# Two mixing stages reordered: the place of GLA's exponent, of three projections and of GLA's norm, and the release of attention's score banks

## What is computed

```python
x = x + 0.5 * mx[2] * swiglu(modulate(rms_norm_2(x), mx[0], mx[1]), ffn1_w1[l], ffn1_w3[l], ffn1_w2[l])
hx = modulate(rms_norm_2(x), mx[3], mx[4]) @ w_in[l]
hz = modulate(rms_norm_2(z), mz[3], mz[4]) @ w_in[l]
mix_x, mix_z = token_mixing(hx, hz, ..., not last)
x = x + mx[5] * (mix_x @ w_out[l])
x = x + 0.5 * mx[8] * swiglu(modulate(rms_norm_2(x), mx[6], mx[7]), ...)   # z likewise, if not last

def token_mixing(...):            # four mixers, 256 of the 1024 channels each
    a_x = fourier_mix(px['fourier'])                     # 2D FFT over tokens and 64 channels, real part
    b_x = neighborhood_attention(na_q, na_k, na_v, kz_na, vz_na, na_rpb)   # 4 heads of 64, window + context, bias
    ox_gla, _, _ = bidir_gla(*gla_prepare(px, *gates), s_f, s_b)   # gated linear attention, both directions
    c_x = gla_output(ox_gla, px['gla_r'], gla_norm)      # rms norm over a head, times silu(r)
    d_x = block_attention(qx_gqa, keys of x and z, values of x and z)      # 4 heads, 2 kv heads, rope
    return concatenate([a_x, b_x, c_x, d_x])             # in layer 0 the same for z
```

## Time and profile before

| | us |
|---|---|
| median of three runs | 3559.2 |
| lowest, highest | 3558.4, 3567.6 |
| the profiled execution | 3562.57 |
| its span, first to last instruction | 3560.7 |
| TensorE busy | 3386.7 |
| VectorE, ScalarE, GpSimd busy | 1622.9, 580.0, 43.8 |
| mean granted clock of TensorE | 0.977 |

### The profile page before, as it was taken

One profiled execution on the slowest core, in us unless ns is written; L12 is line 12 of the kernel. 1 busy time (PEld: TensorE's weight loads), 2 busy tenths in 40 slices (PEclk: granted clock), 3 DMA queues, 4 the chain that ended last, 5 costly groups with the idle time before them and its releaser, 6 DMA issues.

```text
span 3560.7 us, 41820 instructions
## 1 busy us (share of the span) xinstructions
PE 3386.7 (95%) x16652; PEld 2770.6 (78%) x16652; DVE 1622.9 (46%) x3349; ACT 580.0 (16%) x1208; POOL 43.8 (1%) x48
## 2 busy tenths in 40 slices
PE   8999999999999999999999778999999999987999
PEld 7887888888888888788885444688888888664888
DVE  4667223145682232365563643564656556344100
ACT  2121112111211021100003234100011000233100
POOL 0000000000000000000000010000000000020000
PEclk9999999999999999999999889999999999998999
DMA  5777557636775476333322120232322323231454
GB/s 185 216 201 237 170 155 208 165 101 190 213 234 191 145 210 179 93 83 95 83 90 59 52 38 24 63 109 66 95 83 71 107 68 98 55 84 29 130 157 116
DMA packets 655631, 440.69 MB, mean 124 GB/s; under 512 B 24336, under 2 KB 654512, under 8 KB 655312
## 3 DMA queue, kind: packets, MB, share of 16 engines
q1 hardware_dynamic: 652416, 430.28, 41.8%
q0 software_dynamic: 1552, 6.07, 1.0%
q10 hardware_dynamic: 1472, 1.68, 0.1%
HBM read 436.94 MB, written 1.05 MB: 123 GB/s over the span
## 4 chain that ended last, share of the span: by engine, by line
PE 92%; DVE 5%; ACT 2%; issue 1%; DMA 0%; ACTq 0%; DVEq 0%
PE psum L1751 46%; PE psum L1943 22%; PE psum L1966 11%; PE psum L2153 2%; PE psum L1758 2%; PE psum L1888 2%; DVE small L1713 1%; PE psum L2106 1%; PE psum L2135 1%; ACT hh L1123 0%; DVE arena L1628 0%; PE psum L1827 0%; PE psum L1767 0%; PE psum L2047 0%; PE psum L2141 0%
## 5 line engine op out<-in xcount | busy, mean ns | idle before, releaser
L1751 PE MATMUL psum<-hh,ring 128*128 128x256 f32 (+2 forms) x5344 | 1263.9, 395 | 8.3 <-ACT hh L1123 4.8
L1751 PEld LDWEIGHTS psum<-hh,ring 128*128 128x128 f32 (+1 forms) x5344 | 1010.4, 191 | 237.7 <-issue 103.8
L1751 PE MATMUL psum<-arena,ring 128*128 128x256 f32 x1568 | 344.8, 383 | 8.2 <-DVE arena L1487 5.5
L1751 PEld LDWEIGHTS psum<-arena,ring 128*128 128x128 f32 x1568 | 300.8, 192 | 51.8 <-DVE arena L1487 6.3
L1943 PE MATMUL psum<-hh,arena 128*128 128x256 f32 x1056 | 252.1, 382 | 8.8 <-issue 5.8
L1943 PE MATMUL psum<-hh,ring 128*128 128x256 f32 x1056 | 245.9, 386 | 4.6 <-ACT hh L1123 4.0
L1943 PE MATMUL psum<-arena 128*128 128x256 f32 x1056 | 241.4, 382 | 0.0
L1402 DVE SCALAR_TENSOR_TENSOR arena<-arena,par 128x255 f32<-128x255 f32 (+14 forms) x480 | 225.2, 469 | 17.0
L1966 PE MATMUL psum<-arena 128*128 128x256 f32 x1056 | 231.8, 379 | 0.0
L1943 PEld LDWEIGHTS psum<-hh,ring 128*128 128x128 f32 x1056 | 202.6, 193 | 37.2 <-ACT hh L1123 5.1
L1943 PEld LDWEIGHTS psum<-hh,arena 128*128 128x128 f32 x1056 | 201.5, 191 | 37.4 <-issue 9.9
(11 more groups left out here) (259 smaller groups left out, 2858.3 us busy)
## 6 DMA issues: line engine op xcount, KB each, us to landing
ring<-in_ffn_w SPq DMA_DIRECT2D x176, 512.0 KB, 5.1
ring<-in_w_mod SPq DMA_DIRECT2D x72, 1024.0 KB, 7.6
ring<-in_w_in SPq DMA_DIRECT2D x54, 1024.0 KB, 5.3
ring<-in_w_up SPq DMA_DIRECT2D x88, 512.0 KB, 5.3
ring<-in_w_in SPq DMA_DIRECT2D x84, 512.0 KB, 5.2
ring<-in_w_down SPq DMA_DIRECT2D x16, 1408.0 KB, 7.1
ring<-in_ffn_w SPq DMA_DIRECT2D x12, 1536.0 KB, 6.7
ring<-in_ffn_w SPq DMA_DIRECT2D x12, 1280.0 KB, 5.9
```

The source lines that it names most:

```text
L1751: ins = mm(o[0:rows_, 0:T], w[:, k, c0:c0 + rows_], src[:, k, 0:T], start=(k == 0), stop=(k == kt - 1))
```

## The change

It has five parts.

1. `g_exp` for s = 1 moves from the head projections to behind `gv` 1, so behind all head norms. In layer 1 `g_exp` for s = 0 goes there too. In layer 0 `g_exp` for s = 0 moves to behind `g_o` of s = 1 and in front of the Fourier transforms and `na_load`.
2. The `vp` tiles and `fp` are spread. In layer 0: `vp` 0 before `g_kt`; `fp`, `vp` 1 and 2 behind the scores of s = 1; Fourier behind `g_o` of s = 1; `vp` 3 behind the scores of s = 0. In layer 1: `fp` and `vp` 0 before `g_kt`, Fourier behind `g_s0`, `vp` 1 to 3 behind the scores.
3. The four `na_bias` steps move from rounds 2 and 3 of attention to the front of `g_o` of s = 0.
4. `g_n` for s = 0 moves from round 0 to the round behind the last `at`. In that round it stands before the last `at_n`. It gets buffers of its own (`sq_x`, and halves of `sd2`).
5. The exponential frees the score bank; `exp2_done` goes. Units of z put the four transposes of both heads in one bank, copied by one instruction.

`rs` and `sd`, of which the rest of the stage uses 256 columns at most, are cut from 512 columns to 256, which makes room for `sq_x`. The diff, cut to its core:

```diff
+def at_banks(u):
+    return 2 if u[1] == 0 else 1
...
@@ plan_second
         if 2 <= n and order[n - 2] >= 4:
             p.step("nrot", l, n - 2, order[n - 2])
             p.job("nrot", l, n - 2)
-        if n == 4:
-            p.step("g_exp", l, 1)
-        if n == 6 and last:
-            p.step("g_exp", l, 0)
...
-    if not last:
-        gla_scores(1)
...
+    for t in range(2 * TT):
+        p.step("gv", l, t)
+        p.job("gv", l, t, chunk=("w2", l, "glav"))
+        if t == 1:
+            p.step("g_exp", l, 1)
+            if last:
+                p.step("g_exp", l, 0)
+    if last:
+        fourier_in()
+        values(0)
+        gla_state()
+        fourier()
+        gla_scores(0)
+        values(1, 2, 3)
+    else:
+        values(0)
+        gla_state()
         gla_scores(1)
...
-    if not last:
+        fourier_in()
+        values(1, 2)
+        gla_out(1)
         p.step("g_exp", l, 0)
-        gla_out(1)
-    for t in range(2 * TT):
-        p.step("vp", l, t)
-        p.job("vp", l, t, chunk=("w2", l, "v"))
-    gla_scores(0)
+        fourier()
+        gla_scores(0)
+        values(3)
     for i in range(2):
         p.step("rp", l, i)
         p.job("rp", l, i, chunk=("w2", l, "glar"))
     if not last:
         gla_norm(1)
+    for hd in range(4):
+        p.step("na_bias", l, hd)
+        p.job("flip", l, hd)
     gla_out(0)
...
-        if n == 0:
+        if n == len(units):
             gla_norm(0)
         if 1 <= n <= len(units):
             p.step("at_n", l, n - 1)
-        if n in (2, 3):
-            for hd in (2 * n - 4, 2 * n - 3):
-                p.step("na_bias", l, hd)
-                p.job("flip", l, hd)
         if 2 <= n < len(units) + 2:
             p.step("at_t", l, n - 2)
-            for b in range(2):
+            for b in range(at_banks(units[n - 2])):
                 p.job("at_t", l, n - 2, b)
...
+        def gla_buffers(s, pr):
+            if s == 1:
+                return sqb2[:, pr, 0:S], raw2[:, pr, 0:S], sd2[:, pr, 0:S]
+            return sq_x[:, pr, :], raw_x[:, pr, :], sd_x[:, pr, :]
...
@@ ScalarE, at and at_t
-                        do(nc.scalar.activation(p2[:, n % 4, b, 0:nk], bank(job[("at", l, n, b)])[:, 0:nk], ACT.Exp,
-                                                bias=stat2[:, i:i + 1], accum_out=stat2[:, 4 + i:5 + i]),
-                           exp2_done, 2 * m + b + 1)
+                        free(nc.scalar.activation(p2[:, n % 4, b, 0:nk], bank(j)[:, 0:nk], ACT.Exp,
+                                                  bias=stat2[:, i:i + 1], accum_out=stat2[:, 4 + i:5 + i]), j)
...
+                    if at_banks(u) == 1:
+                        j = job[("at_t", l, n, 0)]
                         produced(act, j)
+                        free(nc.scalar.activation(to[:, :, 0:2, :], bank(j).rearrange("p (b k t) -> p b k t", b=2, k=2), ACT.Copy), j)
...
@@ VectorE, at_n
-                        dve.wait_ge(exp2_done, 2 * m + b + 1)
-                        free(nc.vector.reciprocal(stat2[:, 8 + b:9 + b], stat2[:, i:i + 1]), job[("at", l, n, b)])
+                        evacuated(dve, job[("at", l, n, b)])
+                        do(nc.vector.reciprocal(stat2[:, 8 + b:9 + b], stat2[:, i:i + 1]))
```

112 lines of the change are left out of this document (68 added, 44 removed).

## The result

The changed kernel took **3531.5 us** (median of 4 runs, 3530.9 to 3534.9). The kernel before took 3562.2 in the same comparison (4 runs, 3558.4 to 3567.6). The ratio is 0.991, with a 95% interval of 0.990 to 0.993. The profiled execution took 3530.9 us, against 3562.6 of the one before: 31.7 us won, where the working said 31.3.

The account below looks back on a forecast made before the run. TensorE, busy 95% of the span, bounds the kernel; only its waits and low clock can yield time. Layer 0's 12.9 and layer 1's 18.4 us make 31.3 won, from median 3559.2 to 3528 (spread 3521 to 3534; with rivals 3514 to 3543).

Parts of the forecast that it names:

- Term 1: Layer 0 up to the second GLA scores: head-norm waits give way to one before the transposes of k; 4.3 us won.
- Term 2: Layer 0, Fourier: TensorE waits some 4.3 us for ScalarE's exponent of s = 0, where it waited 0.79; 3.5 us lost.
- Term 3: Layer 0, from rp to attention's first transposes: 14.6 us behind rp's end, 10.1 us won.
- Term 4: Layer 0, attention loop and tail: earlier-freed banks shorten the loop, the norm lengthens the tail; 59.7 us become 57.7, 2.0 won.
- Layer 1 (19.0 and -0.6): Layer 1: 19.0 us won up to attention's first transposes as the 8.26 us wait goes; 0.6 lost in loop and tail.
- A: Attention loops: ScalarE and handoffs, not the banks, set them, gaining some 5 and 3 us; 3538 us, chance 0.15.
- B: Layer 0: the stall moves, clock stays low through the scores, Fourier waits 8 us; 3537 us, chance 0.09.
- C: Tails and loops: no low clock in the tails (5 us), nothing lost at handoffs (3.5); 3519.5 us, chance 0.14.
- D: Attention loops: longer waits at their start leave the clock at 1.2 GHz throughout, 54 us lost; 3582 us, chance 0.04.

Follow-up runs that it names:

- the banks run: Changed kernel with score banks freed by the reciprocal again and two banks and two copies for every unit's transposes: 3543.4 us, ratio to before 0.9958.
- the last kernel: Changed kernel with three v tiles before layer 0's transposes of k, exponent of s = 0 beside the last v tile, norm of s = 0 in two pieces: 3495.2 us.

## Why the prediction was right, and where it wasn't

The forecast was 3528 and the time 3531.5, inside the forecast's own spread. On the scale of the profiled executions the sum was 31.3 and the measured gain 31.7; on that of the medians the gain was 30.8. 3.0 of the 3.5 us between 3528 and 3531.5 come from putting the sum on the median of 3559.2, where the comparison had 3562.2. That the sum came within 1 us is partly luck. The runs of before scatter over 9 us, their median was 3559.2, 3561.1 and 3558.7 in the later comparisons, and the interval of the ratio allows a gain of 26 to 37 us. The mechanism is borne out by the stretches: four times within 0.7 us of the forecast. Inside the first of them, though, errors of up to 1.7 us cancelled, and `out` of layer 0 lost 2.5 that had no term of its own.

**Term 1 (4.3): 4.8 measured.** The wait was 10.63 us (10.8 forecast), the state took 3.67 (3.78 taken from layer 1). The Fourier projection starts 57.2 us behind head projection 6 and started 56.8 behind it before; 5.2 us of v tile are done by then. From the transposes to that projection it takes 18.1 us where it took 15.9: the slow start cost 2.2, not 2.8.

**Term 2 (-3.5): -5.2 measured.** This is the term whose size was wrong. The wait of 4.43 was forecast as 4.3. What was missing is the half clock behind it: the transform took 6.37 us. I had charged that loss to every other new wait but not to this one. It cost 2.7, and about 1 us came back elsewhere in the stretch, half of it in `fp` (14.40, 14.88 before). The kernel with the exponent one tile earlier got 6.6 us back, against 3.5 by my term.

**Term 3 (10.1): 11.5 measured**, of which 1.5 is rp itself (15.42 before, 13.90 now). No term had that; it is no effect of the edit that I can show. From its end to the first transposes it is 14.7 us, 14.6 forecast, and VectorE's first maximum starts 11.0 us behind `rp`, as worked out.

**Term 4 (2.0): 2.5 in the stretch, but 0.1 with `out`.** The loop up to the end of the last exponential is 40.6 us (41.4 forecast) and the tail 16.5 (13.8 + 2.5). The short units inside the loop came out otherwise than walked: seven intervals between their exponentials take 18.6 us, 2.65 each and not 2.25, and took 23.5 before, 3.35 each and not 2.9. The saving of 0.7 per unit is the one forecast; the level of both was 0.4 too low. The rest of the loop then took some 3.6 us less than walked, so that the two errors cancelled. The 2.5 were meant to hold all the work at half clock. The transposes (1.97 us, where the kernels without that wait show 1.09) and the output (3.68, where 1.95 is) took 2.6 by themselves, and `out` behind them 2.5 more (57.6 against 55.1). The banks part was worth 11.5 and 4.6 us of T, by the loops alone 10.1 and 4.3; my loops of before and after differ by 10.2 and 7.6.

**Layer 1 (19.0 and -0.6): 19.2 and 0.1.** The sizes are right. The working named the cover (gv, fp and a v tile), and that is what did it. The other sentence, that the head norms no longer stop there, was wrong: they had not stopped TensorE in layer 1 before, and with the exponent put back the stretch is the same. The forecast was right in spite of it, since that sentence had no time of its own in the sum. Loop and tail are 22.2 and 16.5 us, where 23.1 and 16.3 were forecast.

**The rivals.** A is refuted by the banks run, B by the sizes: Fourier waited 4.4 us and not 8, and terms 1 and 2 together are -0.4 and not -8. C's half, no low clock in the tails, is refuted by the rows at 0.50; of its other half, 3.5 us for handoffs, 0.8 and 0.9 came. D didn't come: the loop's stretch is granted 1.00. By the Trainium skill (TensorE: Matmul & The Clock Gate, PE-mode transpose) a loop of transposes would have stayed low. Neither loop shows it: both have 1.00, in the earlier trace rows and in the row of 2126 to 2146 above.

**The two pages' rules.** A table load is 1.28 us also in the new tail, and the root starts behind it without a gap:

```profile
2159.38 1.28 ACT L1287 ACT_TABLE_LOAD   x1
2160.68 0.98 ACT L1287 ACTIVATE arena<-psum,small 128x256 f32<-128x256 f32 x2
```

The Trainium skill's drain of 1380 ns (ScalarE: Activation LUTs, What ACT_TABLE_LOAD costs) is not in these rows, and the sum without it was the nearer one. Its rule on bursts and waits (TensorE: Matmul & The Clock Gate, HAM oscillation) agrees with what followed the new waits: 3.67 us for the state in place of 1.99, 6.37 for the transform in place of 3.69, and 0.50 at the end of the tail.

**What stays open.** The line "all the rest" of the first table is a sum of parts that nearly cancel. 3.9 us are won ahead of projection 6 of layer 0, where nothing was changed (it is at 1971.90 before, 1967.98 after, 1974.65 in the last kernel). 2.5 are lost in `out` of layer 0, 1.1 between it and projection 6 of layer 1, and 1.7 behind the start of `out` of layer 1. So the two stages themselves gave 30.5 of the 31.7 us. Slower runs of one kernel have a lower mean granted clock (0.975 to 0.976 at 3567 us, 0.977 to 0.978 at 3559, both the kernel before); I didn't find what decides it.

## What to carry to other kernels

When an edit moves a slow step of another engine, ask two things: who stands behind the step on its own engine, and which independent work stands in front of whoever waits for its result. In layer 0 the first decided most (6.8 us, against 4.2 for the spread). In layer 1 only the second counted: 12 us of projections in front of the waiter removed 11.6 us, and the step's place among the head norms was worth nothing. A norm moved to the other end of a loop is not gone; split it, with its roots where their table is loaded or ScalarE waits, and its products behind the last work that others wait for. Count with each new long wait of TensorE (4.4, 6.0 and 10.6 us here) the slow work behind it, 1.7 to 2.7 us for the first steps, and 2.5 more in `out` of layer 0.
